# Index queries kept in SBUF, rings of three and four PSUM banks for transposes, and a re-paced search in a hybrid attention layer

## What is computed

```python
h = concat(meta, x)
proj = rms_norm(h, g_mix_pre) @ w_in            # q,k,v of both branches, index q,k,w, two gates
# branch 1, stick-breaking attention, 8 heads of 64
z = q_sb @ k_sb.T / 8
a = exp(log_sigmoid(z) + sum_{later visible keys} -softplus(z))   # strictly causal
o_sb = a @ v_sb
# branch 2, sparse attention, 8 heads of 64: an indexer (8 heads of 32) picks 256 keys per query
score = sum_h w_idx[h] * relu(q_idx[h] @ k_idx.T)
sel = top_k(score, 256)                          # causal
o_ds = softmax(q_ds @ k_ds[sel].T / 8) @ v_ds[sel]
merged = sigmoid(g_sb) * (o_sb @ w_branch_sb) + sigmoid(g_ds) * (o_ds @ w_branch_dsa)
h = h + rms_norm(merged @ w_out, g_mix_post)
h = h + rms_norm(relu(rms_norm(h, g_mlp_pre) @ w_mlp_in) ** 2 @ w_mlp_out, g_mlp_post)
```

## Time and profile before

| | us |
|---|---|
| median of 3 runs | 2052.66 (2051.76 to 2054.29) |
| the profiled execution | 2053.31 |
| its span, first to last instruction | 2051.5 |
| TensorE busy | 1817.6 |
| VectorE busy | 1074.3 |
| ScalarE busy | 652.7 |
| mean granted TensorE clock, share of 2.4 GHz | 0.948 |

### The profile page before, as it was taken

The page is one execution under the profiler, slowest core; times in us unless marked ns, Lnnn a source line. Parts: engine busy times, 40 slices in busy tenths (PEclk is TensorE's granted clock), DMA queues, the critical chain, the costliest instruction groups (busy, mean ns, idle before and its releaser), DMA issues. The chain is left out here.

```text
span 2051.5 us, 25668 instructions
## 1 busy us (share of the span) xinstructions
PE 1817.6 (89%) x10056; PEld 1539.7 (75%) x10056; DVE 1074.3 (52%) x1911; ACT 652.7 (32%) x1283; POOL 335.5 (16%) x135
## 2 busy tenths in 40 slices
PE   4778579788899899997888998999999999999997
PEld 3677568668787677776777787888888888888885
DVE  4265378897999963357777443441322222232226
ACT  4244323233343344454555223240211203022022
POOL 0110010110111011100000244030413304032130
PEclk9998889898899999998889999999999999999999
DMA  4423332343323323332311344220202102021122
GB/s 149 139 87 106 109 96 71 104 107 87 100 65 86 97 66 102 92 97 63 94 39 36 125 142 164 93 92 11 83 11 72 54 30 82 11 72 42 42 84 121
DMA packets 63983, 170.53 MB, mean 83 GB/s; under 512 B 7720, under 2 KB 22376, under 8 KB 63864
## 3 DMA queue, kind: packets, MB, share of 16 engines
q1 hardware_dynamic: 63864, 168.90, 27.0%
HBM read 126.47 MB, written 42.41 MB: 82 GB/s over the span
## 5 line engine op out<-in xcount | busy, mean ns | idle before, releaser
L574 PE MATMUL bk<-x_hi,w_hi 128*128 128x512 f32 (+2 forms) x832 | 321.8, 387 | 10.6 <-PEq L262 6.3
L574 PE MATMUL bk<-x_lo,w_hi 128*128 128x512 f32 (+2 forms) x832 | 309.4, 372 | 0.0
L574 PE MATMUL bk<-x_hi,w_lo 128*128 128x512 f32 (+2 forms) x832 | 308.0, 370 | 0.0
L243 POOL TENSOR_TENSOR w_lo<-w_raw,w_hi 128x1024 fp32r<-128x1024 f32 x53 | 131.3, 2477 | 782.2 <-ACT w_hi L239 782.2
L1240 PE MATMUL bank<-m_hi,w_hi 128*128 128x512 f32 x512 | 199.6, 390 | 0.0
L1240 PE MATMUL bank<-m_hi,w_lo 128*128 128x512 f32 x512 | 199.3, 389 | 0.0
L1240 PE MATMUL bank<-m_lo,w_hi 128*128 128x512 f32 x512 | 199.3, 389 | 0.0
L1329 ACT ACTIVATE relu<-bank 128x1024 f32<-128x1024 f32 x32 | 33.0, 1030 | 504.8 <-PE bank L1240 504.8
L574 PEld LDWEIGHTS bk<-x_hi,w_hi 128*128 128x128 f32 x832 | 167.1, 201 | 29.2 <-POOL w_lo L243 6.4
L892 DVE TENSOR_SCALAR_CACHE_REDUCE sel<-sc,st_bits 128x272 bf16<-128x272 f32 (+6 forms) x217 | 183.2, 891 | 1.0
L635 PE MATMUL bk<-idf,a_buf 128*128 128x128 f32 (+1 forms) x704 | 107.3, 283 | 82.3 <-DVE pt_lo L989 79.6
(11 more groups left out here) (171 smaller groups left out, 3561.5 us busy)
## 6 DMA issues: line engine op xcount, KB each, us to landing
w_raw<-w_units SPq DMA_DIRECT2D x99, 512.0 KB, 3.8
raw<-w_units SPq DMA_DIRECT2D x24, 512.0 KB, 3.5
k_hi<-k_d SPq DMA_DIRECT2D x32, 260.0 KB, 5.8
k_lo<-k_d SPq DMA_DIRECT2D x32, 260.0 KB, 6.3
q_st<-q_d SPq DMA_DIRECT2D x16, 512.0 KB, 3.8
g_d<-stage_hi SPq DMA_DIRECT2D x32, 256.0 KB
gate<-g_d SPq DMA_DIRECT2D x16, 512.0 KB, 4.6
v_raw<-v_d SPq DMA_DIRECT2D x16, 260.0 KB, 7.0
```

Of the source, the lines that this page charges most:

```text
L243: pool.tensor_tensor(w_lo[:, s], w_raw[:, s], w_hi[:, s].bitcast(F32), ALU.subtract).then_inc(lo_done, 1)
L574: mm = pe.matmul(pj[b][:, 0:c1 - c0], w[:, s, kt, :], a[:, kt, c0:c1], start=kt == 0 and k == 0, stop=kt == KT - 1 and k == 2)
```

## The change

- `qi` is eight tensors, one for each index head, in SBUF that later stages use. `ki` and `load_qi(0)` are issued before `store(8)`, `load_qi(h)` behind `store(7 + h)`, without a wait. The index scores begin at chunk 10 (the slots go from 158 to 152). `load_head(1)` waits for the last index score, as its buffers overlap three of the eight.
- Transposes go to banks 4, 5 and 6, from step 66 on also to bank 0, always the one used longest ago; the wait is for the last use of that bank.
- Outputs use bank 7 alone in stick-breaking jobs, 7 and 1 in sparse jobs. Scores use banks 2 and 3 throughout.
- `SEARCH_NS`, the yields, `dve_work` and `work` get other numbers.
- `rest_output(j-4)` stands behind `rest_weights(j-2)`.

```diff
+def tp_take(key, j):
+    ring = (4, 5, 6) if j < NJ // 2 + 2 else (4, 5, 6, 0)
+    TPN[key] = len(TP_BANK)
+    TP_BANK.append(min(ring, key=lambda b: max([n for n, x in enumerate(TP_BANK) if x == b], default=-1)))
...
+TP_PREV = [max([m_ for m_ in range(n_) if TP_BANK[m_] == b_], default=None) for n_, b_ in enumerate(TP_BANK)]
+def o_bank(j):
+    return 7 if j < NJ // 2 or j % 2 == 0 else 1
...
-slots_ = [(n_, k_) for n_ in range(W_AT, NC_STEP) for k_ in range(KT)][2:]
+slots_ = [(n_, k_) for n_ in range(FIRST_CHUNK[4], NC_STEP) for k_ in range(KT)]
...
-    return 0.89 * keys[0] + 0.9 * keys[1] + 1.41 * keys[2]
+    return 0.89 * keys[0] + 0.9 * keys[1] + 1.41 * keys[2] + 850
...
-    return (3.42 * KEYS[JOBS[j - 1][2]] if j >= 1 else 0) + (1.33 * KEYS[JOBS[j - 2][2]] if j >= 2 else 0) + 250
+    ends = sum(UNITS[CHUNK[n_][0]][0] not in ("v", "g") for part_ in ENDS[j] for n_ in part_)
+    return (3.42 * KEYS[JOBS[j - 1][2]] + 300 if j >= 1 else 0) + (1.33 * KEYS[JOBS[j - 2][2]] + 200 if j >= 2 else 0) + 560 * ends
...
-SEARCH_NS = 300e3
+SEARCH_NS = 278e3
...
-        qi = at("qi", [P, 2, SEQ], F32R, O_A + 8 * T + 4096)
+        qi = [at(f"qi{h}", [P, SEQ], F32R, off) for h, off in enumerate(
+            [O_A + 8 * T + 4096, O_A + 8 * T + 8192, O_V, O_V + 4096, O_PT + 4 * T + 8192] + [O_QK + QK_SET + 4096 * k for k in range(3)])]
...
                     elif g == 1:
                         sp.wait_ge(tp_ready, TPN["v", 0, 1] + 1)
+                        sp.wait_ge(s_ready, HI * NCH)
...
                     for n in range(FIRST_CHUNK[u], LAST_CHUNK[u] + 1):
-                        store(n)
                         if n == FIRST_CHUNK[3]:
...
-                            for h in range(2):
-                                load_qi(h)
-                        for h in range(2, HI):
-                            if QI_AT[h] == n:
-                                sp.wait_ge(s_ready, (h - 1) * NCH)
-                                load_qi(h)
+                            load_qi(0)
+                        store(n)
+                        if 0 <= n - FIRST_CHUNK[3] < HI - 1:
+                            load_qi(n - FIRST_CHUNK[3] + 1)
...
+                def turn_bank(n):
+                    if TP_PREV[n] is not None:
+                        pe.wait_ge(tp_free, TP_PREV[n] + 1)
+                    elif TP_BANK[n] < 2:
+                        bank_read(NC_ALL - 2 + (TP_BANK[n] + NC_ALL) % 2)
...
-                        if t == SB:
-                            if z >= 2:
-                                pe.wait_ge(zs_used, z - 1)
-                            dst = bk[2 + z % 2][:, 0:c1 - c0]
-                        else:
-                            z -= NZ_SB
-                            if z >= 4:
-                                pe.wait_ge(zd_used, z - 3)
...
-                            dst = bk[(2 + z) % 4][:, 0:c1 - c0]
+                        if 2 <= z < NZ_SB + 2:
+                            pe.wait_ge(zs_used, z - 1)
+                        elif z >= 2:
+                            pe.wait_ge(zd_used, z - 1 - NZ_SB)
+                        dst = bk[2 + z % 2][:, 0:c1 - c0]
...
                 def product(j):
-                    if j >= 2:
+                    if j == NJ // 2 + 1:
+                        bank_read(NC_ALL - 2 + (1 + NC_ALL) % 2)
+                    elif j > NJ // 2 + 1:
                         pe.wait_ge(o_free, j - 1)
+                    elif j:
+                        pe.wait_ge(o_free, j)
...
                         for j, b in enumerate(range(1, NB)):
                             op(dve.tensor_scalar(sel[:, BOFF[b]:BOFF[b] + KEYS[b]], sc[:, blk(b)], cand[:, j:j + 1], None, ALU.is_ge, ALU.add,
                                                  accum_out=cnt[:, j:j + 1]))
-                            yield 60 + 1.05 * KEYS[b]
+                            yield 150 + 1.04 * KEYS[b]
...
-                        yield 100
+                        yield 350
...
-                for q in range(2):
-                    dve.memset(tp[q][:], 0.0).then_inc(z_tp, 1)
+                for q in range(3):
+                    dve.memset(bk[4 + q][:], 0.0).then_inc(z_tp, 1)
...
                 for j in range(NJ + 4):
-                    if 4 <= j and JOBS[j - 4][0] == DS:
-                        rest_output(j - 4)
...
                     if 2 <= j < NJ + 2:
                         rest_weights(j - 2)
+                    if 4 <= j and JOBS[j - 4][0] == DS:
+                        rest_output(j - 4)
```

More of the change, by code:

```diff
@@ L415, in build @@
             ki_in, wt_t, wt_done = sem("f_kiin"), sem("f_wtt"), sem("f_wtok")
-            qi_in = [sem("f_qiin0"), sem("f_qiin1")]
+            qi_in = [sem(f"f_qiin{h}") for h in range(HI)]
             s_ready, s_relu, s_acc, search_op = (sem("f_" + n) for n in ("sready", "srelu", "sacc", "search"))
@@ L596, in values @@
                             col = 0 if half else c * DH
-                            mm = pe.transpose(tp[n % 2][0:r, col:col + DH], v_raw[:, c * P:c * P + r], idf[0:DH, 0:DH])
+                            mm = pe.transpose(bk[TP_BANK[n]][0:r, col:col + DH], v_raw[:, c * P:c * P + r], idf[0:DH, 0:DH])
                         mm.then_inc(tp_ready, 1)
@@ L632, in turn @@
                         n = TPN["p", j, k]
-                        pe.wait_ge(tp_free, n - 1)
+                        turn_bank(n)
                         for m, (c, r) in enumerate(tiles):
-                            mm = pe.transpose(tp[n % 2][0:r, m * P:(m + 1) * P], a_buf[:, j % 3, c * P:c * P + r], idf[:])
+                            mm = pe.transpose(bk[TP_BANK[n]][0:r, m * P:(m + 1) * P], a_buf[:, j % 3, c * P:c * P + r], idf[:])
                         mm.then_inc(tp_ready, 1)
@@ L656, in _ @@
                             for i in range(NB):
-                                mm = pe.transpose(ops[0][:, i * HI:(i + 1) * HI], w_t[:, i * P:(i + 1) * P], idf[0:HI, 0:HI])
+                                mm = pe.transpose(bk[7][:, i * HI:(i + 1) * HI], w_t[:, i * P:(i + 1) * P], idf[0:HI, 0:HI])
                             mm.then_inc(wt_t, 1)
@@ L664, in _ @@
                 pe.wait_ge(s_relu, HI * NCH)
-                pe.wait_ge(z_tp, 2)
+                pe.wait_ge(z_tp, 3)
                 values(0)
@@ L752, in round_weights @@
                             act.wait_ge(pv_done, j - 1)
-                        act.copy(pt_hi[:, j % 2, 4 * k:4 * k + m, :], tp[n % 2][:, 0:m * P].rearrange("p (c k) -> p c k", c=m)).then_inc(tp_hi, 1)
+                        act.copy(pt_hi[:, j % 2, 4 * k:4 * k + m, :], bk[TP_BANK[n]][:, 0:m * P].rearrange("p (c k) -> p c k", c=m)).then_inc(tp_hi, 1)
                 def round_values(g):
@@ L769, in output @@
                             act.wait_ge(o_spilled[j % 2], 16 * (j // 2))
-                        act.copy(o_st[:, j % 2], ops[j % 2][0:DH, 0:P]).then_inc(o_free, 1)
+                        act.copy(o_st[:, j % 2], bk[o_bank(j)][0:DH, 0:P]).then_inc(o_free, 1)
                     else:
                         r = DH * (g % 2)
-                        act.copy(o_hi[r:r + DH, g // 2, i * P:(i + 1) * P], ops[j % 2][0:DH, 0:P]).then_inc(oh_done, 1)
+                        act.copy(o_hi[r:r + DH, g // 2, i * P:(i + 1) * P], bk[o_bank(j)][0:DH, 0:P]).then_inc(oh_done, 1)
                 def reload(p):
@@ L880, in select @@
                     op(dve.memset(cur.bitcast(I32), 0))
-                    yield 700
+                    yield 1000
                     settle()
@@ L884, in select @@
                         op(dve.tensor_scalar(sc[:, blk(b)], sc[:, blk(b)], sgn[:, j:j + 1], None, ALU.mult))
-                        yield 60 + 0.6 * KEYS[b]
+                        yield 150 + 0.6 * KEYS[b]
                     settle()
@@ L1003, in rest_output @@
                     dve.wait_ge(oh_done, j + 1 - NJ // 2)
-                    dve.tensor_tensor(o_lo[dst], ops[j % 2][0:DH, 0:P], o_hi[dst].bitcast(F32), ALU.subtract).then_inc(o_free, 1)
+                    dve.tensor_tensor(o_lo[dst], bk[o_bank(j)][0:DH, 0:P], o_hi[dst].bitcast(F32), ALU.subtract).then_inc(o_free, 1)
                 def rest_reload(p):
```

48 lines of the change are left out of this document (21 added, 27 removed).

## The result

The changed kernel takes 1948.43 us (1943.87 to 1949.03, 4 runs) beside 2053.47 us for the kernel before on the same chip: 0.948 of its time, 95% interval 0.946 to 0.950, or -105 us. The forecast was 1958 us (-95), with 1925 to 2003 as its range. The profiled execution took 1947.99 us, its span is 1946.2. One execution of the experiment olo_first took 9698.95 us, far slower than its other three; it is left out, and that median is of three runs.

The account below looks back on a forecast made before the run. The prediction held that two DMA engines bound the first stretch, and that no engine was full in the sparse jobs. Index queries -22, pacing and third bank -34, sparse jobs -39 sum to -95: 2053.3 to 1958 us, range 1925 to 2003.

Parts of the forecast that it names:

- The bound of the first stretch: Up to 258 us: two DMA engines bind, with 242 of 258 us of stores and other transfers; `qi` loads queue there.
- Rival A: First stretch: the stores don't bind and all `qi` waits go, another 36 us, 1922 us; chance 0.08.
- Index queries: Projections with index scores: early `qi` loads into eight buffers gain 22 us (bounds +8 and -58).
- -10.7 - 2 - 3.8: Index part: first `qi` wait 1 us, not 11.7; matmuls at low clock, 2; two DMA engines relieved, 3.8.
- the -5: Between 260 and 270 us, DMA share 0.01: TensorE enters the loop with stores queued, so half of 10 us goes.
- hidden under the stores: First 12 steps of the stick-breaking loop: the gain of pacing and third bank does not show there.
- Search pacing and third bank: 48 steps of the stick-breaking loop, six heads: 429 us for 463, -34 (bounds +53 and -49).
- the 71.5 us a head: Stick-breaking loop: each head takes the clean 69 us plus 2.5 for a VectorE that is 90% loaded.
- Rival B: Stick-breaking heads: the paced search gains nothing and heads stay as they are on average, 1992 us; chance 0.17.
- Sparse jobs: 64 sparse jobs: waits of 38.5 and 6.6 us go, 6 us of short waits come; 213 us for 252, -39.
- C: Sparse jobs gain nothing: granted clock is 0.88 and two score banks take back the gain, 1997 us; chance 0.14.
- D: Sparse jobs: TensorE and VectorE alternate; slower once overlap is under 1.23 us a job, 2131 with none; chance 0.04.

Follow-up runs that it names:

- olo_first: The changed kernel with `rest_output(j-4)` put back at the top of the step: 1964.52 us, 0.957 of the kernel before.
- before_split: The kernel before with each store of k, q and v cut into one DMA a head, nothing else: 2000.24 us, 0.975 of the kernel before.
- after_split: The changed kernel with each store of k, q and v cut into one DMA a head: 1882.00 us, 0.917 of the kernel before.
- before_qi: The kernel before with only the new index part (eight `qi` buffers, early loads, new slots): 2039.76 us, 0.994 of the kernel before.
- banks_only: The kernel before with only the new banks for scores, transposes and outputs (and `work` + 850): 2020.43 us, 0.985 of the kernel before.
- before_pacing: The kernel before with only the new yields, `SEARCH_NS` and `dve_work`, two transpose banks: 2006.21 us, 0.977 of the kernel before.
- two_qi: The changed kernel with the old index part (two `qi` buffers, old loads and slots): 1964.88 us, 0.957 of the kernel before.

## Why the prediction was right

**The bound of the first stretch** was named rightly. Two DMA engines carried the stores, and `qi` was waited for because it stood behind them; before_split, after_split and before_qi show it from three sides: with the stores cut the waits for `qi` fall to the first one, with the stores cut the changed kernel gains 66 us, and with the waits for `qi` removed but the stores as they were, waits for stores come in their place. Rival A, by which all 47.9 us would go, is out: before_qi gave 14.5. The Trainium skill's rule on the number of engines a copy runs on ("DMA: Bandwidth & Descriptors", the section on the increment by 16) agrees with what cutting the stores did, a DMA share from 0.13 to as much as 1.00.

**Index queries, -22 forecast.** The first wait fell from 11.70 to 0.46 us, as worked out. Up to the third set of `values` the gain is 12.4 + 5.5 = 18 us. The second term is not the index part's, since before_qi has none of it, banks_only 6 us and before_pacing 4. By before_qi and two_qi the index part is worth 14.5 to 16.5 us, and -10.7 - 2 - 3.8 of the forecast is -16.5. The step that failed is the -5, "TensorE will enter the loop with stores queued behind it": from 250 to 260 us the DMA share is 0.02, as empty as the 0.01 before. Stores and scores moved forward together, so the gap moved too. That alone makes the -22 a -17. For pacing and banks the forecast had "hidden under the stores" in the first 12 steps. That was right in the main and wrong by 5.5 us: with the stores cut in both kernels, the change as a whole is worth 132.1 - 115.9 = 16 us there.

**Search pacing and third bank, -34 forecast, -52 measured.** The mechanism was right, and the mis-sized term is the 71.5 us a head. The 2.5 us that a VectorE 90% loaded was to cost on top of 69 is not there: with two transpose banks a late head takes 68.8 us with VectorE busy 35.81 and 69.2 with 63.51, with three it takes 67.7 us with 24.77 and 67.9 with 65.56. The 1.1 to 1.3 us that the third bank takes off such a head were not in the sum. The mean head is 411.3 / 6 = 68.6 us, with VectorE busy 94% (386.29 of 411.30), which is 64 us a head and not 61 to 63. 429 - 411.3 = 18 us is the error. Of the gain some 41 to 43 us are pacing and 8 to 11 the third bank, by which of the two comes first. The search ended at 803 us, not near 840. The shorter heads explain 18 of these 37 us; the rest was never in the forecast's own terms, by which step 60 stood at 378 + 429 = 807. Rival B is out: before_pacing alone gave more than the forecast for both.

**Sparse jobs, -39 forecast, -36 measured.** 64 jobs took 212.7 us for a forecast of 213. The two windows don't begin at the same point: from the first logits (892.7 us before, 824.4 now) to the branches it is 250.1 and 213.3, so 37 of the 252 - 213 = 39 us. That the sum nearly came out is in part luck, for its division did not: it gave 38.5 to the order and 6.6 to the banks as two waits of VectorE, while each edit alone gives 20. It had no term for the clock, and 14 us of this stage's 36 are TensorE's own busy time. The handover of the score banks was priced at 6 us and is 13.6 of TensorE's time, of which a third bank gets 5 back. Rivals C and D are out: the stage became shorter, and its granted clock, which spoke for C, rose from 0.88 to 0.95. D needed an overlap under 1.23 us a job, and it is (180.8 + 186.0 - 212.7) / 64 = 2.4.

**The sum.** The three gains were forecast at 22, 34 and 39 us and measured at 18, 52 and 36: 4 too much, 18 too little, 3 too much. So 1958 us lies 10 us above the result. It would lie 17 above it if the two smaller errors did not hide part of the large one. The four parts alone give 14.5 + 48 + 32 + 16.3 = 111 us for 105 together, so they hardly overlap except in the sparse jobs.

## What to carry to other kernels

A wait names the transfer that came last, not the one that was in the way: look at the DMA share before the wait, and where it stands at two sixteenths for long, look for a copy whose outer dimension is 2 and cut it. Work that is interleaved by booked times must be booked by the measured ones, and then an engine at 94% costs its neighbour little: 68.6 us a head here, where one with VectorE busy 37% took 67.7. In a ring of waits between two engines, measure each edit alone and both together before giving the gain to one of them.

## What the runs showed of the hardware

**Stores.** The same k, q and v went at 51 GB/s with a DMA share of 0.13 when a store had two heads as its outer dimension, and when each head had its own DMA a window among the stores reached a share of 1.00 and 280 GB/s, loads included.

**Such stores hold SyncE too.** In the changed kernel's timeline of SyncE single issues take up to 10 us in the stretch of the stores, where those of the earlier trace rows took 0.5 to 0.6 each. The second row has all issues of weight loads between 95 and 400 us in after_split, shortest, median and longest in ns:

```profile
283.26 10.24 SPq L249 DMA_DIRECT2D w_raw<-w_units  x1
...
L249 SPq DMA_DIRECT2D w_raw<-w_units x19: 577/584/593, 102.1 to 392.1; - x19
```

With the stores cut, no issue of SyncE in this stretch takes over 1.4 us, so the long ones come with the stores on two engines. That a queue was full at those times is a guess that no run shows.

**VectorE behind GpSimd.** In the six heads some multiplications and scans of the stick-breaking weights take 2.3 to 3.2 us, some 2 us longer than others of their shape. The timeline of the changed kernel shows one such multiplication with the usual time, and what stands beside a long one:

```profile
401.54 0.57 DVE L967 TENSOR_TENSOR a_buf<-a_buf,n_buf 128x400 f32<-128x400 f32 x1
...
671.08 2.66 POOL L258 TENSOR_TENSOR w_lo<-w_raw,w_hi 128x1024 fp32r<-128x1024 f32 x1 [16.31 <-ACT w_hi L254]
671.60 2.58 DVE L967 TENSOR_TENSOR a_buf<-a_buf,n_buf 128x400 f32<-128x400 f32 x1
```

The GpSimd operation ends at 671.08 + 2.66 = 673.74 us and VectorE's at 674.18, 0.44 us behind it; at 688.04 it is the same, with 2.70 us for 128x528 (0.71 elsewhere), ending 0.57 us behind a GpSimd operation that began at 687.45. The Trainium skill ("SBUF — State Buffer", the section on two separate sides) says that the two engines share a port pair and that one of them holds it for its whole instruction; the rows fit that. There are 24 such GpSimd operations in the 48 steps, and beside at least 13 of them a VectorE instruction takes some 2 us longer than others of its shape. So an estimated 26 us of VectorE's 386 are standing still. No run here moved them.
